# Retention: queries times sample states for two sequences in one step, in four column groups

## The reference

```python
def step(s, xs):
    qi, ki, vi = xs
    att = jnp.einsum('bhid,bhjd->bhij', qi, ki) * decay_intra
    o = (jnp.einsum('bhij,bhjv->bhiv', att, vi)
         + jnp.einsum('bhid,bhdv->bhiv', qi * q_dec[..., None], s))
    s = s * s_dec[:, None, None] + jnp.einsum('bhjd,bhjv->bhdv', ki * k_dec[..., None], vi)
    return s, o
```

## Time and profile before

| | us |
|---|---|
| runs, median of 3 | 2330.04 |
| runs, lowest and highest | 2323.69, 2330.73 |
| profiled execution | 2336.64 |
| its span | 2334.8 |
| TensorE busy in the span | 1955.0 (84%) |
| VectorE busy | 811.9 (35%) |
| ScalarE busy | 399.1 (17%) |
| POOL busy | 347.9 (15%) |
| mean granted clock of TensorE | 0.904 of full |

### The profile page before, as it was taken

How to read it: one execution, slowest core, us unless ns; L and a number is a source line. 1 busy time by engine, 2 the same in 40 slices (tenths; PEclk the granted TensorE clock), 3 DMA queues, 4 the chain that set the end, 5 groups by cost and what they waited for, 6 DMA issues and landing times. The chain is left out here.

```text
span 2334.8 us, 33151 instructions
## 1 busy us (share of the span) xinstructions
PE 1955.0 (84%) x13455; PEld 1074.2 (46%) x13455; DVE 811.9 (35%) x1670; ACT 399.1 (17%) x884; POOL 347.9 (15%) x472
## 2 busy tenths in 40 slices
PE   5999999999899499945998998899887689669970
PEld 3443433434244344424756756756645534334430
DVE  0123233232332400034346546546544422410007
ACT  1010110001000021223232233233231100011110
POOL 0010110101121210030031031031030003210004
PEclk9999999999799699975998999999886789779995
DMA  9535246251620579978223033033017571069964
GB/s 342 205 106 203 92 135 240 82 180 36 234 89 28 196 267 345 339 276 308 76 88 105 24 98 117 20 102 106 22 57 227 176 212 54 23 224 347 343 253 164
DMA packets 221242, 381.86 MB, mean 164 GB/s; under 512 B 17165, under 2 KB 88469, under 8 KB 221078
## 3 DMA queue, kind: packets, MB, share of 16 engines
q1 hardware_dynamic: 214002, 354.22, 43.6%
q0 software_dynamic: 7104, 25.69, 2.9%
HBM read 305.25 MB, written 74.63 MB: 163 GB/s over the span
## 5 line engine op out<-in xcount | busy, mean ns | idle before, releaser
L545 PE MATMUL bank<-ring,hT 128*128 128x512 f32 x768 | 345.4, 600 | 3.1 <-PEq L262 2.0
L1286 PE MATMUL bank<-hT,ring 128*128 128x272 f32 x1024 | 288.7, 419 | 12.1 <-PEq L869 12.1
L2227 PE MATMUL bank<-ring,exp_xT 128*128 128x512 f32 x512 | 230.5, 604 | 21.1 <-issue 17.3
L545 PEld LDWEIGHTS bank<-ring,hT 128*128 128x128 f32 x768 | 142.3, 191 | 188.6 <-issue 185.9
L1286 PEld LDWEIGHTS bank<-hT,ring 128*128 128x128 f32 x1024 | 189.6, 198 | 59.3 <-issue 25.9
L2803 PE MATMUL bank<-ring,oT 128*128 128x512 f32 x384 | 173.6, 613 | 13.3 <-DMA oT<-oT_spill 12.7
L2227 PEld LDWEIGHTS bank<-ring,exp_xT 128*128 128x128 f32 x512 | 96.0, 192 | 136.3 <-issue 131.3
L2803 PEld LDWEIGHTS bank<-ring,oT 128*128 128x128 f32 x384 | 75.1, 197 | 107.2 <-issue 94.1
L1283 PE MATMUL bank<-ring,hT 128*128 128x512 f32 x256 | 117.7, 605 | 0.0
L2246 PE MATMUL bank<-ring,exp_aT 128*128 128x512 f32 x256 | 115.4, 593 | 1.6 <-ACT exp_aT L2281 1.6
L2316 DVE TENSOR_TENSOR exp_a<-bank,exp_sg 128x256 f32<-128x256 f32 x32 | 13.6, 424 | 278.3 <-ACT exp_sg L2299 278.3
(11 more groups left out here) (441 smaller groups left out, 2549.4 us busy)
## 6 DMA issues: line engine op xcount, KB each, us to landing
ring<-in_moe_w_gu_dram SPq DMA_DIRECT2D x32, 2048.0 KB, 9.4
ring<-in_w_ada_dram SPq DMA_DIRECT2D x24, 2048.0 KB, 8.9
ring<-in_moe_w_down_dram SPq DMA_DIRECT2D x32, 1024.0 KB, 12.0
ring<-in_ret_w_in_dram SPq DMA_DIRECT2D x8, 2048.0 KB, 13.4
ret_Ss<-in_state_ret_dram SPq DMA_DIRECT2D x32, 512.0 KB, 5.0
out_dram<-ret_Ss SPq DMA_DIRECT2D x32, 512.0 KB, 3.4
expert_outputs<-exp_y SPq DMA_DIRECT2D x32, 512.0 KB, 4.7
ring<-in_dn_w_in_dram SPq DMA_DIRECT2D x8, 2048.0 KB, 8.7
```

The costliest lines, as they stand in the source:

```text
L545: last = pe.matmul(ps[u % 2][:, :], core.hT[:, k, tok(t)], core.ring[:, w % RING, k, :], start=(k == 0), stop=(k == KD - 1))
L1286: mm = pe.matmul(ps[U % 2][:, 0:HALF], core.ring[:, w % RING, k, c * P:(c + 1) * P], core.hT[:, k, half * HALF:(half + 1) * HALF], start=( ...
L2227: last = pe.matmul(ps[v][:, :], xT[:, v, k, :], wgu[v][:, k, :], start=(k == 0), stop=(k == KD - 1))
```

## The change

The products of two sequences are taken out of `seq` and put into a step of their own, `pair` i, for sequences 2i and 2i + 1. It waits for both states, and then issues four products, first half 0 of both sequences and then half 1, which fall in column groups 0, 2, 1, 3. The updates (L613, L815) stay one by one in `seq`. Pair 0 stands before `seq` 0 in round 7, pair 1 before `seq` 2 in round 8, pair 2 between `seq` 3 and `seq` 4 in round 9, and pair 3 before `seq` 6 in round 11. Each pair signals `so_parts` (four times per head instead of once); VectorE waits for it before it overwrites a state. The waits on `o_done` and `qds_done` go with pair 0, the one on `st_done` stays with `seq` 0. SP's and POOL's steps are the same as before.

```diff
--- before.py
+++ after.py
@@ -442,9 +442,9 @@
 
         STEPS = {0: [("turn", 0), ("turn", 1)], 1: [("turn", 2), ("turn", 3)], 2: [("turn", 4), ("scores", 0)],
                  3: [("chunk", 0)], 4: [("chunk", 1), ("norm", 0)], 5: [("chunk", 2), ("norm", 1)],
-                 6: [("out", 0), ("chunk", 3), ("norm", 2)], 7: [("seq", 0), ("out", 1), ("norm", 3), ("seq", 1)],
-                 8: [("seq", 2), ("out", 2)], 9: [("seq", 3), ("seq", 4)], 10: [("seq", 5), ("out", 3)],
-                 11: [("seq", 6), ("seq", 7)], 12: [("fold", 4), ("norm", 4)], 13: [("out", 4)]}
+                 6: [("out", 0), ("chunk", 3), ("norm", 2)], 7: [("pair", 0), ("seq", 0), ("out", 1), ("norm", 3), ("seq", 1)],
+                 8: [("pair", 1), ("seq", 2), ("out", 2)], 9: [("seq", 3), ("pair", 2), ("seq", 4)], 10: [("seq", 5), ("out", 3)],
+                 11: [("pair", 3), ("seq", 6), ("seq", 7)], 12: [("fold", 4), ("norm", 4)], 13: [("out", 4)]}
 
         def program(project, step):
 
@@ -589,22 +589,27 @@
                             last = pe.matmul(ps[2 + a][:, :], kd[:, i, a * P:(a + 1) * P], v[:, h % 2, i, :],
                                              start=True, stop=True)
                         last.then_inc(s["st_ps"], 1)
-                    if what == "seq":
+                    if what == "pair":
                         x = o_unit(h, NPT)
                         o = ps[6 + x % 2]
                         if i == 0:
                             pe.wait_ge(s["o_done"], x - 1)
                             pe.wait_ge(s["qds_done"], h + 1)
+                        for b in (2 * i, 2 * i + 1):
+                            n = DECB * h + b
+                            pe.wait_ge(s[f"ss_in{n % SLOTS}"], 16 * (n // SLOTS + 1))
+                        for a in range(2):
+                            for b in (2 * i, 2 * i + 1):
+                                j = 2 * (b % 2) + a
+                                last = pe.matmul(o[NS * j:NS * (j + 1), :], qds[:, a, b, :],
+                                                 Ss[:, (DECB * h + b) % SLOTS, a, :],
+                                                 start=(i == 0), stop=(i == DECB // 2 - 1), skip_group_check=True)
+                        last.then_inc(s["so_parts"], 1)
+                    if what == "seq":
+                        if i == 0:
                             pe.wait_ge(s["st_done"], 2 * NPT * (h + 1))
                         b = i
                         n = DECB * h + b
-                        pe.wait_ge(s[f"ss_in{n % SLOTS}"], 16 * (n // SLOTS + 1))
-                        for a in range(2):
-                            j = 2 * (b % 2) + a
-                            last = pe.matmul(o[NS * j:NS * (j + 1), :], qds[:, a, b, :], Ss[:, n % SLOTS, a, :],
-                                             start=(b < 2), stop=(b >= DECB - 2), skip_group_check=True)
-                        if b == DECB - 1:
-                            last.then_inc(s["so_parts"], 1)
                         if b > 0:
                             pe.wait_ge(s["ss_done"], 2 * n)
                         pe.wait_ge(s["kds_done"], n + 1)
@@ -663,7 +668,7 @@
                     n = rows(i)
                     if what == "seq" and i == DECB - 1:
                         act.wait_ge(proj, UNITS * h + (4 if h + 1 < H else 3) * NT)
-                        act.wait_ge(s["so_parts"], h + 1)
+                        act.wait_ge(s["so_parts"], DECB // 2 * (h + 1))
                         act.activation(parts[:, :], ps[6 + o_unit(h, NPT) % 2][:, :], ACT.Copy).then_inc(s["so_kept"], 1)
                     if what == "turn":
                         x = NT * h + i
@@ -810,6 +815,7 @@
                     if what == "seq":
                         b = i
                         y = DECB * h + b
+                        dve.wait_ge(s["so_parts"], DECB // 2 * h + b // 2 + 1)
                         dve.wait_ge(s["ss_ps"], y + 1)
                         for a in range(2):
                             dve.scalar_tensor_tensor(Ss[:, y % SLOTS, a, :], Ss[:, y % SLOTS, a, :], sdec[:, 1, h:h + 1],
```

## The result

The changed kernel takes 2365.57 us (median of 4, 2358.92 to 2369.38) against 2330.39: a ratio of 1.0152, 95% interval 1.0121 to 1.0184. Measured again, in six executions, it was 1.0128 (1.0106 to 1.0150). Predicted were 2346.7 us, at most 2358: the direction is right, the size is not. The loss is 35.2 us in the first measurement and about 30 in the second, about twice the 16.7 us of the sum. The profiled execution took 2358.92 us.

A forecast was written before the change was run, and what follows sets the result against it. TensorE was taken to bound heads 0 to 2, with VectorE's update chain right beside it, and state loads the last head. Stalls 4.2 + clock 6 + last head 6.5 = 16.7 us on 2330.04 gave 2346.7 us, range 2336 to 2358.

The forecast's parts named there:

- price of a step of four: Four products in four column groups take 0.98 us, as long as two products of one sequence; bounds 0.96 and 1.96.
- gain of nothing in rounds 7 and 11: Products removed there were hidden in waits for VectorE's update, so removing them gains 0.
- one product in round 10: Products of sequence 5 vanish from round 10 and nothing else is late there: gain 0.98 us per head.
- mechanism of round 9: Pair 2 needs state 5, whose load goes out only after update 2; TensorE waits about 4 us, loss 2.4 us per head.
- (c): Rival: the step of four doesn't overlap in four, 1 us more per pair on the path, 16 us, 2362; chance 0.05.
- term of the clock in round 9: Heads 0 to 2: granted clock falls after the 4 us stalls, 2.0 us per head, +6 us, bounds 0 and 9.6.
- waits of 1.0 and 1.64 us: Sign in the profile after: L613 of sequences 1 and 7 released by VectorE's update after these waits.
- The landing: Round 9: state 5's load lands 4.6 us after issue, at 351.26; bounds 3.8 to 6.9 us.
- The last head: Rounds without projections wait for state loads: +1.3 us if the clock stays up, +7.6 at the low level; taken +6.5.
- the waits 4.2: Heads 0 to 2: round 9 loses 2.4, round 10 gains 0.98, 1.4 us per head, +4.2 us for three.

The follow-up runs named there:

- other data: Changed kernel, but each pair multiplies both sequences' queries with the first one's state, and each update waits for its own state; 1.0010 of the kernel before.
- pair 2 split: Pairs in heads 0 to 2 only, pair 2 undone: products 4 before update 4, products 5 a projection later; last head as before; 1.0002 of the kernel before.
- filled version: Changed kernel with extra dense products of the next projection in the waits of rounds 7, 9 and 11, heads 0 to 2; 1.0057 of the kernel before.

## Why the prediction was wrong

**Right.** The direction and the place: all waits stand where they were forecast, pair 2 of each head and pairs 1 to 3 of the last, released by the load of a state, and the updates of 1 and 7 by VectorE with 0.99 and 1.63 us (forecast 1.0 and 1.64). The price of a step of four: 0.99 (0.98). The gain of nothing in rounds 7 and 11 and of one product in round 10. The mechanism of round 9, shown by the runs with other data and with pair 2 split. The prediction failed in the sizes, above all in what the clock takes after the waits. None of its rivals happened either: (c) has 2362 us, close to what was measured, but its reason, 1 us more for each pair, is not there.

**The term of the clock in round 9 was mis-sized.** I took 2.0 us per head between 1.7 and 3.2. Against the full clock, pair 2 cost 0.87 more, the update 0.95, and the projection 1.9, 1.2 and 2.0: 3.7, 3.0 and 3.8, together 10.5 instead of 6. The analogue that I leaned on, with the earlier trace rows, had one short low stretch, while here it lasted 7 to 10 us. It was also one of the two mild cases of the three waits of that line. The third, in the same trace of the kernel before and of nearly the same length, was followed by a granted clock of 0.50 for 14 us (1251.8 to 1266):

```profile
1251.87 2.07 PE L1484 MATMUL bank<-dn_ue,dn_kds 32*128 32x512 f32 x4 [3.64 <-DVE dn_ue L1961]
...
1254.00:1258.00 4.00, 4.00 (x38) 2.48 (x38) 2.99 (x11) 0.36 (x2) 0.00 (x0) 0.50 0.00 0
```

The light products after the wait ran in the low stretch and didn't end it, as the last head had shown already; I should have taken the upper bound and more of the projection with it.

**The clock in the other waits was left out.** I forecast the waits of 1.0 and 1.64 us and gave them the price 0. In round 11 of head 2 the clock fell after such a wait: 2.0 for the update and 9.41 instead of 7.13 us for the projection, 3.2 us. The filled version supports that the waits are the cause. Which of them is hit changes from run to run and from kernel to kernel (16 of 36, above).

**The landing.** From the start of update product 3 to pair 2 are 5.4 us (353.22 to 358.67; 5.40 and 5.27 in heads 0 and 2) against the forecast 5.0, as the load took 4.9 and not 4.6: 1.1 us in all.

**The last head** cost 9.7 instead of 6.5. The period at the low clock was 10.64 us (622.76 to 633.40), forecast 10.4, and then 11.73 (to 645.13), since the load of state 7 took 5.7 us and not 4.6. Another 0.4 us is in the first wait, 3.97 instead of 3.6. The working at the low clock gave 7.6, and I chose less than it, though the clock fell in the very wait of 3.6 us that I had named. As the last head of the same code varies by some us, the single shares are read from one pair of profiles and no more.

Sum for heads 0 to 2: the waits 4.2 + 1.1, the clock 10.5 + 3.2, less 1.7 for a fall in head 2 that the kernel before had and the changed one had not (0.53 between 577.9 and 581), make 17.3 of the measured 17.8 us.

**The range.** The upper end, 2358, is more than its terms give: 4.2 + 9.6 + 7.6 with landings half a microsecond longer come to about 2354. The 27.5 us of the four lengths would lie just at 2358; the other 7.7 us of the first measurement are explained by no row here. The next stage starts 28.7 us later, where 17 were forecast.

## What to carry to other kernels

Grouping products whose operands arrive one by one moves the need for the last operand forward; look up which event issues its load, and leave the landing time between that event and the group. Products that lie inside a wait for another engine are worth nothing when removed, and the hole they leave can cost more than itself in granted clock (after 1.6 us of waiting up to 3.3 us here, after 4 us 3.0 to 3.8), so price each new hole with the low clock through the next dense stretch. Once the updates were spread so that no hole was left in the sequence steps, packing six of eight sequences in three heads brought 0.4%, and the new order another 0.3%.

## What was not expected

The overlap of four column groups was forecast from the earlier trace rows; how it stands to one full-size product was not worked out. Four products took 0.99 us, where one full-size product takes 0.89: a packing of 4 x 0.89 / 0.99 = 3.6. The Trainium skill (TensorE: Matmul & The Clock Gate, Measured speedup vs the span model) has 2.38 for three column tiles; these rows are nearer to the full factor.

Idle times of 1.0 to 1.7 us between light products were enough for the granted clock to fall in some heads (0.58 in the 4 us after a wait of 1.04 us in the run with other data), and filling them with three extra sets of dense products, which are thrown away, made the kernel 0.7% faster than leaving them empty. The Trainium skill (TensorE: Matmul & The Clock Gate, HAM oscillation — how this bites in real kernels) tells of falls after long waits for transfers between bursts of matmuls; the trace agrees for the waits of 4 us (0.50 after them), and shows falls after shorter ones too. Whether a given short wait is followed by a fall could not be foretold from any row here; that stays open.
